# Two products per weight block instead of three: the high half of a block meets both input halves in one product of 512 columns

## What is computed

```python
# first block
q, k, v, z, xbc, dt_raw = jnp.split(rms_norm(x, g_mix) @ w_in, splits, axis=-1)
x = x + jnp.concatenate([dilated_attention(q, k, v), ssd_mixer(z, xbc, dt_raw)], axis=-1) @ w_out
x = x + cross_attention(rms_norm(x, g_cross), rms_norm(mem, g_mem), w_cq, w_ckv, w_co)
x = x + jnp.square(jax.nn.relu(rms_norm(x, g_mlp) @ w_up)) @ w_down      # 2048 -> 8192 -> 2048
# second block
c_q, c_kv, k_r, x_r, y_r, ga, gr = split_columns(rms_norm(h, attn_norm) @ w_in_2)
h = h + (sigmoid(ga) * mla_branch(c_q, c_kv, k_r) + sigmoid(gr) * rglru_branch(x_r, y_r)) @ w_out_2
h = h + peer_ffn(rms_norm(h, ffn_norm))      # w_peer_q, top 16 of 16 x 16 pairs, rows of peer_u and peer_v
h = h + sigmoid(rms_norm(h, ple_norm) @ w_ple_gate) * (p @ w_ple_proj)
return rms_norm(h, final_norm)
```

## Time and profile before

| | |
|---|---|
| median of 3 runs | 4106.8 us (4105.35 to 4119.67) |
| the profiled execution, its time | 4102.67 us |
| its span, first to last instruction | 4100.9 us |
| TensorE products busy | 2564.1 us (63%), 19730 records |
| DVE busy | 2921.1 us (71%), 3488 records |
| ACT busy | 1309.2 us (32%) |
| POOL busy | 1082.3 us (26%) |
| mean granted TensorE clock | 0.812 |

### The profile page before, as it was taken

How to read it: one execution, slowest core, us unless ns; L and a number is a source line. 1 busy time by engine, 2 the same in 40 slices (tenths; PEclk the granted TensorE clock), 3 DMA queues, 4 the chain that set the end, 5 groups by cost and what they waited for, 6 DMA issues and landing times.

```text
span 4100.9 us, 50118 instructions
## 1 busy us (share of the span) xinstructions
PE 2564.1 (63%) x19730; PEld 2455.5 (60%) x19730; DVE 2921.1 (71%) x3488; ACT 1309.2 (32%) x1780; POOL 1082.3 (26%) x516
## 2 busy tenths in 40 slices
PE   8999798999999999899998986400000000000028
PEld 8888687999999999899996986400000000000028
DVE  5667755654455458654655658899999999999985
ACT  4355444553454445544454442300000000000023
POOL 0000000000000000000000001377767778888850
PEclk9999899999999999999999998755555555555569
DMA  6433243555555564455451547899999999999974
GB/s 216 131 121 114 72 130 118 173 183 186 179 185 185 179 196 145 150 182 183 152 186 43 185 150 288 299 352 355 353 349 353 351 349 400 420 421 418 421 289 133
DMA packets 187579, 952.96 MB, mean 232 GB/s; under 512 B 20816, under 2 KB 21072, under 8 KB 121424
## 3 DMA queue, kind: packets, MB, share of 16 engines
q0 software_dynamic: 73728, 536.90, 33.7%
q1 hardware_dynamic: 112464, 407.68, 31.0%
q10 hardware_dynamic: 1152, 5.17, 0.3%
HBM read 947.58 MB, written 2.10 MB: 232 GB/s over the span
## 4 chain that ended last, share of the span: by engine, by line
PE 54%; DVE 28%; POOL 11%; issue 3%; ACT 3%; DMA 1%; DVEq 0%; ACTq 0%; SPq 0%; POOLq 0%
PE ps L420 53%; POOL BIG L408 9%; DVE HF L1959 8%; DVE BIG L1943 7%; POOL HF L408 2%; DVE HL L1403 2%; DVE BIG L1407 1%; DVE HF L1943 1%; DVE TMP L1403 1%; DVE BIG L1403 1%; DVE TMP L1407 1%; PE ps L424 1%; ACT BIG L909 0%; DVE TMP L1897 0%; DVE TMP L1890 0%
## 5 line engine op out<-in xcount | busy, mean ns | idle before, releaser
L420 PE MATMUL ps<-HS,HL 128*128 128x256 f32 x11936 | 1528.5, 288 | 68.5 <-DVE HL L1403 51.7
L420 PEld LDWEIGHTS ps<-HS,HL 128*128 128x128 f32 x11936 | 1492.9, 196 | 83.8 <-DVE HL L1403 55.6
L408 POOL DMA_INDIRECT BIG<-in_peer_u,CS x211 | 408.9, 1938 | 2717.3 <-DVE CS L1411 2470.9
L1403 DVE TENSOR_TENSOR HL<-RAW,HL 128x1024 fp32r<-128x1024 f32 (+1 forms) x772 | 939.5, 1217 | 222.9 <-ACT HL L915 160.5
L915 ACT CAST HL<-RAW 128x1024 fp32r<-128x1024 f32 (+1 forms) x772 | 805.1, 1043 | 632.2 <-PE ps L420 587.7
L424 PE MATMUL ps<-CON,HF 128*128 128x128 f32 x32 | 7.3, 373 | 1333.1 <-DVE HF L1959 1332.1
L424 PEld LDWEIGHTS ps<-CON,HF 128*128 128x128 f32 x32 | 5.4, 193 | 1335.4 <-issue 1293.3
L420 PE MATMUL ps<-BIGR,HL 128*128 128x256 f32 x5680 | 745.2, 285 | 1.5 <-DVE BIGR L1403 1.5
L420 PEld LDWEIGHTS ps<-BIGR,HL 128*128 128x128 f32 x5680 | 707.9, 192 | 7.8 <-issue 3.7
L1943 DVE CUSTOM_DVE_ANT_0 BIG<-BIG 128x2048 f32<-128x2048 f32 x211 | 483.7, 2292 | 39.9 <-DMA BIG<-in_peer_u,CS 19.6
L1959 DVE SCALAR_TENSOR_TENSOR HF<-BIG,GA,HF 128x2048 f32<-128x2048 f32 x204 | 479.6, 2351 | 22.3 <-DMA BIG<-in_peer_v,CS 1.0
(11 more groups left out here) (160 smaller groups left out, 1763.2 us busy)
## 6 DMA issues: line engine op xcount, KB each, us to landing
RAW<-in_w_up SPq DMA_DIRECT2D x128, 512.0 KB, 3.7
RAW<-in_w_down SPq DMA_DIRECT2D x128, 512.0 KB, 4.2
RAW<-in_w_out SPq DMA_DIRECT2D x64, 512.0 KB, 3.4
RAW<-in_w_qk SPq DMA_DIRECT2D x32, 512.0 KB, 4.3
RAW<-in_w_xbc SPq DMA_DIRECT2D x32, 512.0 KB, 3.3
RAW<-in_w_xr SPq DMA_DIRECT2D x32, 512.0 KB, 3.4
RAW<-in_w_yr SPq DMA_DIRECT2D x32, 512.0 KB, 3.5
RAW<-in_w_gr SPq DMA_DIRECT2D x32, 512.0 KB, 4.2
```

The source lines that it names most:

```text
L408: e.indirect_dma_start(out=ROWS[slot], out_offset=None, in_=A["peer_" + table], in_offset=bass.IndirectOffsetOnAxis(ap=EX[:, i, 16 * h + k ...
L420: return e.matmul(o, l, r, start=start, stop=stop, skip_group_check=True)
L1403: v.done(e.tensor_tensor(o, a, b, op), sig)
```

## The change

For matrices without `tokens` each triple becomes a pair. The high weights meet the high and the low input half in one product of 512 columns (`PAIR` gives the two halves as one access pattern of two runs of 256), written over the whole bank: the left half gathers high by high, the right half high by low. The low weights by the high inputs go into the left half as before. So the two halves of the bank must be added on emptying. The product with low inputs and the other one keep their order k by k.

```
-                                mm(o, wh[:, w], xh, first, False)
-                                mm(o, wh[:, w], xl, False, False)
+                                mm(bank(L, c), wh[:, w], xl, first, last)
                                 p = mm(o, wl[:, w], xh, False, last)
...
+            def halves_at(x, k, tokens=False):
+
+                y = PAIR[x][:, :, k * T:k * T + T]
+                return y[:, 1 if x == "mxa" else 0, :], y[:, 1, :] if tokens else y
...
+            def high_out(o, L, c):
+                s.wait_ge(s_mm, L.done(c))
+                copy(o, bank(L, c)[:, 0:T], (s_part, SUMMED[L.name] + c + 1))
...
+            def summed(o, L, c, sig=None, rows=128):
+
+                v.wait_ge(s_mm, L.done(c))
+                copy(o, bank(L, c)[0:rows, 0:T])
+                tt(o, o, bank(L, c)[0:rows, T:2 * T], ALU.add, sig)
+
             def scaled(o, L, c, sig=None, rows=128):
-                v.wait_ge(s_mm, L.done(c))
-                tt(o, bank(L, c)[0:rows, 0:T], RX[0:rows, :], ALU.mult, sig or sig_bank(L, c))
+                summed(o, L, c, None, rows)
+                tt(o, o, RX[0:rows, :], ALU.mult, sig or sig_bank(L, c))
...
-                tt(X[:, c, :], X[:, c, :], bank(L, c)[:, 0:T], ALU.add, sig_bank(L, c))
+                tt(X[:, c, :], X[:, c, :], bank(L, c)[:, 0:T], ALU.add)
+                tt(X[:, c, :], X[:, c, :], bank(L, c)[:, T:2 * T], ALU.add, sig_bank(L, c))
...
-                    v.wait_ge(s_mm, up.done(c))
-                    stt(buf[:, 0, :], bank(up, c)[:, 0:T], 0.0, RX, ALU.max, ALU.mult, sig_bank(up, c))
+                    summed(buf[:, 0, :], up, c)
+                    stt(buf[:, 0, :], buf[:, 0, :], 0.0, RX, ALU.max, ALU.mult, sig_bank(up, c))
...
+            def low_out(o, L, c):
+                v.wait_ge(s_part, SUMMED[L.name] + c + 1)
+                tt(o, o, bank(L, c)[:, T:2 * T], ALU.add, sig_bank(L, c))
+
+            dense(L["w2_uq"], lambda c: low_out(QN[:, c, :] if c < 16 else QP[:, c - 16, :], L["w2_uq"], c))
...
-                tt(GA_[:, c, :], GA_[:, c, :], bank(L["w2_ao"], c)[:, 0:T], ALU.mult, sig_bank(L["w2_ao"], c))
+                summed(CX, L["w2_ao"], c, sig_bank(L["w2_ao"], c))
...
+                tt(GA_[:, c, :], GA_[:, c, :], CX, ALU.mult)
...
+                while pq[0] < 2 * h + 2:
+                    yield
                 v.wait_ge(*sig_score(SCORE["score"] + h))
```

More of the change, by code:

```diff
@@ L107 @@
 RXN = {"g_mix": 1, "g_cross": 3, "g_mlp": 4, "attn_norm": 5, "ffn_norm": 6, "ple_norm": 7}
+SUMMED = counted([("w2_uq", 24), ("w2_uk", 16), ("w2_pp", 16)])
 NORMED = counted([(n, 16) for n in ("g_mix", "g_cross", "g_mlp", "attn_norm", "ffn_norm", "ple_norm")])
@@ L749, in tensor @@
                 dense(L[f"w_up{half}"], normed("g_mlp"))
-                dense(L[f"w_down{half}"], cut_by(hid, s_hid, lambda k: 32 * half + k + 1),
+                dense(L[f"w_down{half}"], cut_by("hid", s_hid, lambda k: 32 * half + k + 1),
                       residual("attn_norm") if half else None)
@@ L798, in tensor @@
             g_low = low_norms()
-            dense(L["w2_rnn_o"], cut_by(hs, s_ys, lambda k: k // 4 + 1), None, g_low)
+            dense(L["w2_rnn_o"], cut_by("hs", s_ys, lambda k: k // 4 + 1), None, g_low)
             drain(g_low)
-            dense(L["w2_uq"], cut_by(cqs, s_lowcut, lambda k: 1 if k == 0 else 2 if k < 4 else 3))
+            dense(L["w2_uq"], cut_by("cqs", s_lowcut, lambda k: 1 if k == 0 else 2 if k < 4 else 3))
             def evac_k2(c):
@@ L806, in evac_k2 @@
                     rope2(SCORE["qp"] + c // 2, QP[:, c // 2, :])
[L808 removed]
+            low = cut_by("cks", s_lowcut, lambda k: 4 if k == 0 else 5)
             dense(L["w2_uk"], low, evac_k2)
@@ L828, in tensor @@
             drain(pipeline(mla(h) for h in range(16)))
-            dense(L["w2_ao"], cut_by(hs, s_os, lambda k: k // 4 + 1))
-            dense(L["w2_out"], cut_by(mix, s_mix, lambda k: k + 1), residual("ffn_norm"))
+            dense(L["w2_ao"], cut_by("hs", s_os, lambda k: k // 4 + 1))
+            dense(L["w2_out"], cut_by("mix", s_mix, lambda k: k + 1), residual("ffn_norm"))
             norm_end("ffn_norm")
@@ L873, in tensor @@
             drain(g_sc)
-            dense(L["w2_pp"], cut_by(pin, s_pin, lambda k: 1))
+            dense(L["w2_pp"], cut_by("pin", s_pin, lambda k: 1))
             for j in range(8):
@@ L894, in evac_pg @@
                     gated(c - 1)
-            dense(L["w2_pg"], cut_by(hg, s_nlo, lambda k: NORMED["ple_norm"] + k + 1), evac_pg)
+            dense(L["w2_pg"], cut_by("hg", s_nlo, lambda k: NORMED["ple_norm"] + k + 1), evac_pg)
             gated(15)
@@ L1280, in scalar @@
             bank_done(L["w2_rnn_o"], 15)
[L1282 to L1292, removed]
+            def high_out(o, L, c):
+                s.wait_ge(s_mm, L.done(c))
+                copy(o, bank(L, c)[:, 0:T], (s_part, SUMMED[L.name] + c + 1))
+            dense(L["w2_uq"], lambda c: high_out(QN[:, c, :] if c < 16 else QP[:, c - 16, :], L["w2_uq"], c))
+            dense(L["w2_uk"], lambda c: high_out(K2[:, c, :], L["w2_uk"], c))
             def evac_v2(c):
@@ L1357, in scalar @@
             copy(pin[0], PTF, (s_phi, 1))
[L1359 to L1363, removed]
+            dense(L["w2_pp"], lambda c: high_out(PRJ[:, c, :], L["w2_pp"], c))
             for n in range(16):
@@ L1735, in evac_ck @@
             def evac_ck(c):
-                v.wait_ge(s_mm, L["w_ck"].done(c))
-                tt(CK[:, c, :], bank(L["w_ck"], c)[:, 0:T], KEEP[:, 0, :], ALU.mult, sig_bank(L["w_ck"], c))
+                summed(CK[:, c, :], L["w_ck"], c)
+                tt(CK[:, c, :], CK[:, c, :], KEEP[:, 0, :], ALU.mult, sig_bank(L["w_ck"], c))
             v.wait_ge(s_ofree, 16)
@@ L1837, in evac_yo @@
             def evac_yo(c):
-                v.wait_ge(s_mm, L["w2_rnn_o"].done(c))
+                summed(XR[:, c, :], L["w2_rnn_o"], c)
                 v.wait_ge(s_gate, c + 1)
-                tt(XR[:, c, :], GR[:, c, :], bank(L["w2_rnn_o"], c)[:, 0:T], ALU.mult, sig_bank(L["w2_rnn_o"], c))
+                tt(XR[:, c, :], GR[:, c, :], XR[:, c, :], ALU.mult, sig_bank(L["w2_rnn_o"], c))
             g_low = low_norms()
@@ L1844, in vector @@
             drain(g_low)
-            dense(L["w2_uq"])
+            def low_out(o, L, c):
+                v.wait_ge(s_part, SUMMED[L.name] + c + 1)
+                tt(o, o, bank(L, c)[:, T:2 * T], ALU.add, sig_bank(L, c))
+            dense(L["w2_uq"], lambda c: low_out(QN[:, c, :] if c < 16 else QP[:, c - 16, :], L["w2_uq"], c))
             def evac_k2(c):
+                low_out(K2[:, c, :], L["w2_uk"], c)
                 if c % 2 == 0:
@@ L2009, in vector @@
             tt(pin[1], PTF, pin[0].bitcast(F32), ALU.subtract, (s_pin, 1))
-            dense(L["w2_pp"])
+            dense(L["w2_pp"], lambda c: low_out(PRJ[:, c, :], L["w2_pp"], c))
             drain(g_ex)
```

31 lines of the change are left out of this document (16 added, 15 removed).

## The result

| | before | after |
|---|---|---|
| median | 4106.11 us (16 runs, 4103.65 to 4120.11) | 4122.14 us (16 runs, 4111.71 to 4129.98) |
| the profiled execution, its span | 4100.9 us | 4115.5 us |
| products of TensorE, records | 19730 | 13858 |
| DVE busy | 2921.1 us | 3191.1 us |

The ratio after to before is 1.0025, interval 1.0013 to 1.0036: no change by the bound of 0.5%, where a gain of 1.4% was forecast. By either number it is no change. The time lies outside the range.

What follows compares the result with a forecast made beforehand. TensorE was taken to bound most matrix stretches, DVE w_xbc, w2_xr and w_pq to the experts, then the gathers. -86 - 22 + 49.5 = -58.5 against 4102.67 gave 4044, stated as 4048 us for the median; range 4015 to 4097.

Steps and rivals of the forecast that it cites:

- What a triple costs: TensorE's products: a triple takes 360 ns, a pair 336 with the 512 product's weight load hidden, 24 ns saved.
- the 86 us for 3600 triples: Stretches bound by TensorE other than w_up, among them w_down, w_qk and w2_gr: 24 ns saved per triple, -86 us.
- Rival 1: TensorE's products: the 13 ns are a fixed cost per product, 347 ns a pair; 4095 us; chance 0.09.
- 49.5: Stages where DVE is the bound or nearly, and ends of layers: exposed cost of added evacuation work, +49.5 us together.
- Rivals 2 and 3: 2: the 120 ns goes with columns, nothing saved, 4156 us, chance 0.07; 3: loads hide wholly, 4009 us, chance 0.06.
- rival 4: Stages where DVE is near the bound: its added work is exposed in full, +95 us; 4093 us; chance 0.12.
- The gap rule: Trainium skill's figure for TensorE: a pair would save only 2.5 ns, 12 us in all; estimated 4145 us, no separate chance.
- The evacuation: DVE's emptying of banks: 0.92 us more for 252 chunks, 0.46 for 136; 294 us of work, mostly beside TensorE.
- 0.46 us operations for short chunks: w_z, w_ck, w_co, w2_uk, w2_yr, with some 30% DVE slack: 3, 2, 1.5, 2 and 2 us, +10.5 together.

Runs made afterwards that it cites:

- The products by themselves: A separate kernel of only float32r product streams on an idle core, sizes and layouts varied, nothing of the reference computed: 226.7 ns per 512-column product.
- the sums alone: Against the kernel before: three products of 256 columns kept, the second into the bank's right half, halves added on emptying; 4172.76 us, ratio 1.0146.
- the products in groups: Against the kernel with pairs only where DVE has slack: each block's wide products first, then its narrow ones; 4069.8 us, run again 4068.05 us.

## Why the prediction was wrong

**What a triple costs: the step that failed.** The text said of the 13 ns over the columns "I take the weight load for it", and so priced a pair at 336 ns, 24 saved. A pair takes 346.7 or 353.3 ns, and 9.4 to 9.9 are saved in the mean. The products by themselves show the 13 ns in every float32r product of every size, and 7 of them at most go with a shorter load. It put the 512 product at 216 to 220 ns from a row of plain float32; it takes 227 in a row of its own, 230 to 241 in a pair. Half clock hides the 13 ns whatever they are (a pair takes 427 + 213 there, just its columns), so the rows of loads and of half clock, which "both point to the load", don't: neither tells the length of a load from a fixed cost, and the row that gave 216 is of another type. So the 86 us for 3600 triples became, at 9.4 to 9.9 ns, an estimated 35 us: this is the mis-sized term. The rhythm at 353 stood in no case of the forecast; it halves what is saved wherever it rules.

**Rival 1** had the mechanism, at a chance of 0.09, and 12 us less than before, where the profiled execution has 15 more. Of these 27 us 10 are the slow rhythm (189 of 559 groups, 6.7 ns on their share of 4624 triples), 5 are the costs over 49.5, and with the sums alone w_qk, w_cq, w_up and w2_low, which were counted as covered, are 1.7, 2.4, 3.3 and 1.4 us longer, 9 in all. Three are left. Rivals 2 and 3 are out: a pair is 347 to 353 ns, neither 360 nor 325. So is rival 4: w_z, w2_yr and w2_uk lose 0, 0.2 and 1.4 us.

**The gap rule.** "TensorE: Matmul & The Clock Gate" of the Trainium skill, section "Back-to-back issue gap", gives N / 2.4 + 2.5 ns for an isolated product. The bf16 stretch here agrees with it (216 and 109 ns). Float32r doesn't: 120, 173.5 and 226.7. Columns and a constant fit these three too, with 13.3 ns as the constant; the prediction took a mechanism of its own instead.

**w_up.** Forecast DVE-bound at 5.42 us a chunk, 22 us saved; it is TensorE-bound at 5.55, and 9.6 us were saved in the two halves. DVE's chain was sized rightly (5.35), so this is the same mistake as above.

**The evacuation.** Each extra operation costs 0.46 us, as forecast. Taken by itself, with the sums alone, this work lengthens the kernel by 68 us against the 49.5 of the sum; in the changed kernel the faster products give part of that back in the same stages. That the net 55 us came near 49.5 is partly luck: too low prices stand beside too high ones (w_z and w2_yr, 3 and 2 us forecast, lost 0 and 0.2). w_pq lost 12.5 us (13 forecast), w_xbc 9.8 (10), w2_xr 7.8 (9). Low were:
- w_ck, 4.0 for 2: about all of 4 x 0.92 us is exposed.
- w_co, 7.6 for 1.5: 16 x 0.46 = 7.4, exposed in full. Its chunks have four triples each, so DVE's operations a chunk (the sums into X, the low half of the scaled X for the next layer, and the subtraction for each unit of weights) outlast the products: a unit of two chunks takes DVE 4.46 us (its subtractions begin at 723.59 and 728.05), and TensorE took 2 x 1.86 before. PE and DVE of the changed kernel there:

```profile
730.31 1.68 PE L427 MATMUL ps<-BIGR,HL 128*128 128x512 f32 x8 [0.52 <-DVE X L1403]
...
735.13 0.62 PE L427 MATMUL ps<-BIGR,HL 128*128 128x512 f32 x2 [0.87 <-DVE X L1403]
```

```profile
729.84 0.42 DVE L1403 TENSOR_TENSOR X<-X,ps 128x256 f32<-128x256 f32 x1
730.36 0.49 DVE L1407 SCALAR_TENSOR_TENSOR HS<-X,VEC,HS 128x256 fp32r<-128x256 f32 x1
730.95 0.88 DVE L1403 TENSOR_TENSOR X<-X,ps 128x256 f32<-128x256 f32 x2
```

  TensorE waits for the bank that the second addition frees, 2.5 us in four waits, and at the end of the layer 3.5 us (0.3 before) for ACT's squares of X, which come behind the same additions. "0.46 us operations for short chunks" was seen in the prediction, but priced by a mean share of slack of the stage.
- w2_pp, 6.7 for 4. DVE of the changed kernel, the last unit and the return to the dots, against the earlier trace rows:

```profile
2643.84 1.23 DVE L1403 TENSOR_TENSOR HL<-RAW,HL 128x1024 fp32r<-128x1024 f32 x1
2645.17 1.47 DVE L1403 TENSOR_TENSOR BIG<-BIG,ps 128x256 f32<-128x256 f32 x3
2647.06 0.42 DVE L1403 TENSOR_TENSOR BIG<-BIG,ps 128x256 f32<-128x256 f32 x1 [0.42 <-ACT BIG L924]
2647.62 2.29 DVE L1958 CUSTOM_DVE_ANT_0 BIG<-BIG 128x2048 f32<-128x2048 f32 x1
```

  The dots begin 16.8 us after the first product (2630.81) where it was 10.5: 6.3 us later. A unit has four chunks of two triples and takes 3.74 us (2645.17 - 2641.43, the same addition one unit earlier), because TensorE, ACT's copy and DVE's addition now take turns; the forecast let DVE stay only until TensorE's old end.

**Not foreseen and small:** w2_rnn_o, 2.9 us, of DVE (5.5 with the sums alone). TensorE waits there for the low half of the weights, HL, which DVE makes: 5.4 us in two waits, 3.2 before. Why these two and no others grow is not shown.

## What to carry to other kernels

When an edit rests on the cost of an instruction size that the trace doesn't show, measure that size in a kernel of twenty lines before the edit is made; a row of another data type, or one at half clock, doesn't stand for it. An edit that saves on one engine and costs on another is not one edit but as many as there are stages: here it was worth -0.8% in the matrices where DVE has slack (-1.1% with the products in groups) and +0.3% in all. In stages of short chunks the emptying engine's operations count one by one, whatever its busy share is over the stage. A cheaper way to add the two halves of a bank was not tried here.

## What the runs showed of the hardware

- A float32r product with a new load of 128 weight columns costs its columns at 2.4 GHz and 13.3 ns: 120, 173.5 and 226.7 ns for 256, 384 and 512 columns. Bf16 has 3 ns over its columns. At the half clock the 13 ns don't show (213 and 427 ns).
- A stream of float32r products of 512 and 256 columns in turn has two steady rhythms, 346.7 and 353.3 ns a pair, on an idle core too. One kernel's first w_down gained 4.3 us in one execution and 7.7 in another. What selects the rhythm stays open.
- It makes no difference whether the 512 columns are one run in SBUF or two of 256 (226.7 and 227.1 ns).
- A fall of TensorE's clock at one place (w2_uv) lasted 7 us in one execution and 41 in another of the same program, and its stage was 14 us longer in the second, as much as the effects that were looked for. A stage by stage comparison shows it at once; the medians don't.
